# Where the tensors of x, y and h begin in the memory of a decoder-trunk kernel

## What is computed

```python
h = x + 0.5 * swiglu(rms_norm(x, g_ffn1), w_ffn1_gu, w_ffn1_down)      # inner width 2816
u = rms_norm(h, g_mix)
q, k, v, zg, r, us5 = split(u @ w_in)
o    = gated linear attention of q, k, v, zg (chunked recurrence), normed, times silu(r)
o_s5 = diagonal state-space model of us5, gelu, gated
h = h + concat(o, o_s5) @ w_out
h = h + cross_attend(rms_norm(h, g_cross), mem_k, mem_v, w_cq, w_co)
h = h + 0.5 * swiglu(rms_norm(h, g_ffn2), w_ffn2_gu, w_ffn2_down)
y = rms_norm(h, g_final)
```

## The kernel before

| tensor | begins at byte | past a multiple of 128 | past a multiple of 64 |
|---|---|---|---|
| mean_d | 6048 | 32 | 32 |
| gains | 6560 | 32 | 32 |
| eps, one | 6752, 6784 | 96, 0 | 32, 0 |
| h | 6816 | 32 | 32 |
| xh, xl | 25248, 43680 | 32 | 32 |
| yh, yl | 62112, 80544 | 32 | 32 |
| raw | 98976 | 32 | 32 |
| wh, wl | 115360, 123552 | 32 | 32 |
| acc, sq, R, gua, mst | 131744 and on | 32 | 32 |
| AR | 148224 | 0 | 0 |

## Time and profile before

### The profile page before, as it was taken

How to read it: one execution, slowest core, us unless ns; L and a number is a source line. 1 busy time by engine, 2 the same in 40 slices (tenths; PEclk the granted TensorE clock), 3 DMA queues, 4 the chain that set the end, 5 groups by cost and what they waited for, 6 DMA issues and landing times.

```text
span 1282.0 us, 24086 instructions
## 1 busy us (share of the span) xinstructions
PE 1261.7 (98%) x10151; PEld 1218.5 (95%) x10151; DVE 857.1 (67%) x1061; ACT 531.3 (41%) x803; POOL 353.9 (28%) x411
## 2 busy tenths in 40 slices
PE   7999999999999999999999999999999999999997
PEld 6999999999999999999899997599999999999997
DVE  4986479847885636558565437479995589637953
ACT  6644145511224422574443324246553255414543
POOL 0026723288893201000002100032330133102321
PEclk9999999999999999999999999999999999999999
DMA  6233323263223442125333756322332323323322
GB/s 182 81 96 90 91 85 99 83 137 91 74 65 94 91 81 65 51 69 154 119 89 93 232 197 223 122 83 66 100 99 83 99 83 99 91 83 91 87 63 74
DMA packets 221084, 129.94 MB, mean 101 GB/s; under 512 B 22256, under 2 KB 213280, under 8 KB 220960
## 3 DMA queue, kind: packets, MB, share of 16 engines
q1 hardware_dynamic: 217024, 123.83, 33.8%
q10 hardware_dynamic: 3952, 4.58, 1.1%
HBM read 121.42 MB, written 5.78 MB: 99 GB/s over the span
## 4 chain that ended last, share of the span: by engine, by line
PE 92%; DVE 4%; ACT 2%; issue 1%; DMA 1%; SPq 0%; ACTq 0%; DVEq 0%
PE PS L736 89%; PE PS L1361 1%; DMA AR<-in_x_prompt 1%; PE PS L806 0%; ACT wh L1500 0%; ACT gua L1649 0%; DVE Hs L2452 0%; DVE xl L2139 0%; PE PS L1338 0%; DVE AR L2780 0%; PE PS L953 0%; PE PS L1447 0%; DVE ARr L2134 0%; DVE yl L2233 0%; DVE wl L2027 0%
## 5 line engine op out<-in xcount | busy, mean ns | idle before, releaser
L1500 ACT ACTIVATE wh<-raw 128x1024 fp32r<-128x1024 f32 (+1 forms) x126 | 130.1, 1032 | 373.7 <-PE PS L736 373.1
L736 PE MATMUL PS<-yh,wh 128*128 128x288 f32 x960 | 205.6, 296 | 0.0
L736 PE MATMUL PS<-yl,wh 128*128 128x288 f32 x960 | 204.7, 295 | 0.0
L736 PE MATMUL PS<-yh,wl 128*128 128x288 f32 x960 | 204.6, 295 | 0.0
L2027 DVE TENSOR_TENSOR wl<-raw,wh 128x1024 fp32r<-128x1024 f32 (+1 forms) x126 | 154.9, 1229 | 63.7 <-ACT wh L1500 62.3
L736 PE MATMUL PS<-xh,ARr 128*128 128x288 f32 x792 | 174.1, 297 | 0.4 <-ACT sq L1583 0.2
L736 PE MATMUL PS<-xh,wh 128*128 128x288 f32 x736 | 164.4, 305 | 0.1
L736 PE MATMUL PS<-xh,wl 128*128 128x288 f32 x736 | 158.1, 297 | 0.0
L736 PE MATMUL PS<-xl,wh 128*128 128x288 f32 x736 | 157.9, 296 | 0.0
L736 PEld LDWEIGHTS PS<-yh,wh 128*128 128x128 f32 x960 | 154.1, 189 | 1.5 <-DVE yl L2705 0.8
L736 PEld LDWEIGHTS PS<-yh,wl 128*128 128x128 f32 x960 | 154.3, 189 | 0.0
(11 more groups left out here) (378 smaller groups left out, 2183.5 us busy)
## 6 DMA issues: line engine op xcount, KB each, us to landing
raw<-in_w_ffn_gu SPq DMA_DIRECT2D x88, 512.0 KB, 3.9
raw<-in_w_ffn_down SPq DMA_DIRECT2D x32, 512.0 KB, 3.9
raw<-in_w_in SPq DMA_DIRECT2D x16, 512.0 KB, 4.0
raw<-in_w_ckv SPq DMA_DIRECT2D x16, 512.0 KB, 3.8
raw<-in_w_ffn_down SPq DMA_DIRECT2D x16, 384.0 KB, 3.4
Hs<-in_cache_mem_k SPq DMA_DIRECT2D x6, 1024.0 KB, 6.5
raw<-in_w_out SPq DMA_DIRECT2D x8, 512.0 KB, 4.0
raw<-in_w_cq SPq DMA_DIRECT2D x8, 512.0 KB, 4.3
```

Source lines behind the costliest of these rows:

```text
L736: return e.matmul(out, lhsT, rhs, start=start, stop=stop, **kw)
L1500: e.activation(wh[:, n % 2, 0:K * P], raw[:, n % 4, 0:K * P], ACT.Copy).then_inc(w_hi, 1)
```

## The change

The two small constants change their places in the list of tensors. `eps` (32 bytes with rounding) goes ahead of `mean_d`, and `one` (32 bytes) goes from ahead of `h` to behind `raw`. No instruction is added, removed or moved, and no operand changes its size or pattern.

```diff
+        eps = sb("eps", [P, 1])
         mean_d = sb("mean_d", [P, P])
         gains = sb("gains", [P, 6, KD])
-        eps = sb("eps", [P, 1])
-        one = sb("one", [P, 1])
         h = sb("h", [P, KD, T])
         Xs = alias("Xs", 2 * KD * T)
         xh = sb("xh", [P, KD, T], F32R)
...
         yh = sb("yh", [P, KD, T], F32R)
         yl = sb("yl", [P, KD, T], F32R)
         raw = sb("raw", [P, 4, KD * P])
+        one = sb("one", [P, 1])
         wh = sb("wh", [P, 2, KD * P], F32R)
         wl = sb("wl", [P, 2, KD * P], F32R)
```

## The result

| | before | after |
|---|---|---|
| median, 17 runs each | 1284.57 us (1282.56 to 1286.4) | 1286.92 us (1285.42 to 1287.68) |
| ratio | | 1.0016, 95% interval 1.0010 to 1.0022 |
| span of the profiled execution | 1282.0 us | 1285.2 us |

The account below looks back on a forecast made before the run. TensorE's distances between matmul starts were taken as the bound. 2.0 (units) + 5.8 + 0.7 - 1.3 (dense) = 7.2 us off the 1282.0 us span gave 1274.8, with 2.8 for the median 1277.6 us; range 1267 to 1287.5.

Parts of the forecast that it names:

- The bound: Whole kernel: TensorE busy 98% of the span, so the distances between matmul starts make up nearly all the time.
- The third part: All other work on shifted tensors, on ScalarE, VectorE and the loads: counted at nothing.
- What the rows say of starts: Products of a unit: the moving operand's 32 bytes cost 1.6 ns or more a matmul, the stationary operand's nothing.
- The first part: Units: 1188 matmuls go from 133.3 to 131.7 ns, 2.0 us less; 792 streaming from AR unchanged.
- The second part: dense: most matmuls go to 131.7 ns, 5.8 and 0.7 us less; 768 at 130.0 ns lose 1.3 us.
- (c): Rival: dense at 0/32 settles in the slow state, 133.3 ns, throughout; 1285.3 us, chance 0.11.
- (a): Rival: dense falls into the lower rhythm, 130.0 ns, everywhere; 1269.9 us, chance 0.17.
- (d): Rival: operands starting differently within 64 bytes cost time, so dense goes to 134.2 ns; 1289.9 us, chance 0.13.
- (b): Rival: the start doesn't matter and dense keeps its rhythms; 1284.8 us, chance 0.11.
- The rule cited against the change: SBUF reads in 16-byte lines; starts of 32 and 0 both give 72 lines a row, so nothing changes: 1284.8 us.

Follow-up runs that it names:

- maps: Test streams appended behind the last matmul of the kernel before, over pairs of starts of streamed tensor and weights; 131.7 to 133.5 ns a matmul.
- e8: Kernel before with AR alone 128 bytes further on; 1286.71 us, ratio 1.0017.
- e9: Kernel before with eps and one both behind raw, so x, y, h and raw begin 64 bytes earlier; 1281.62 us, ratio 0.9976.
- e2: Kernel before with only yh, yl, raw (and Hs) on a multiple of 128, AR 128 bytes further on; 1286.16 us, ratio 1.0008.
- e5: Kernel before with wh and wl 64 bytes further on, and AR therefore 128; 1282.73 us, ratio 0.9986.
- e3: Kernel before with only h, xh, xl (and Xs) moved to a multiple of 128; 1286.34 us, ratio 1.0012.
- e4: Changed kernel with wh and wl also on a multiple of 128; 1286.29 us, ratio 1.0010 against the kernel before.

## Why the prediction was wrong, point by point

**The bound** was read rightly: TensorE's distances between starts set the time, its two longest waits are 5.2 and 2.5 us, against 5.5 and 2.5 in the earlier trace rows, and nothing on the other engines moved. ScalarE's row and the loads of `raw` of the earlier trace rows read as before (1062 ns against 1059, 3.8 us against 3.9), and VectorE's rows are at 757 and 756 ns again:

```profile
L1500 ACT ACTIVATE wh<-raw 128x1024 fp32r<-128x1024 f32 x110 | 116.8, 1062 | 337.8 <-PE PS L736 337.7
```

```profile
raw<-in_w_ffn_gu SPq DMA_DIRECT2D x88, 512.0 KB, 3.8
```

The third part, counted at nothing, was right.

**The step that failed is the one under "What the rows say of starts"**: that the moving operand's 32 bytes cost 1.6 ns and the stationary one's nothing, read from the products of one unit, and carried over to `dense` ("the pairing of those last two products"). The maps show `dense` at 0/32 and at 32/32 at one pace (133.3 and 133.1 ns), and the kernel does too. In the units the reading fails as well: after the change, products with every operand on a multiple of 128 run at 131.8 and at 133.4 ns side by side, and in e8, where every start within 128 bytes stayed as it was, the last two products went from 132.0 to 133.2 ns. So the 1.6 ns between the products of one unit were not the price of a start within 128 bytes.

What the traces fit instead, in the units, is the distance of the two operands within 256 bytes; no run tests it by itself. The two halves of the tokens begin 1152 bytes (4.5 x 256) apart; `dense` streams both in turn, a product of a unit only one. After the change, the four products whose weights begin 128 bytes away from the streamed tensor within 256 (A11, A12, A22, S3) run at 133.3 to 133.6 ns, the three with no distance (S1, S2, S4) at 131.8 to 132.2. Before, A11 and A12 with 96 bytes ran at 132.9 and 133.4, the last two products with 160 bytes at 132.0 to 132.1; in e9 it is A11 and A12 that have 160, at 132.5 to 132.7, and the last two that have 96, at 132.9 and 133.3. It is not the whole of it: S4 has 96 bytes in e2, e5 and e8 and runs at 132.1 to 132.2, and in 6 of the 33 units of before the last two products ran at 133.2 ns from the same places.

**The first part** (units, 2.0 us less) came out as 0.3 us more. The streams of `xh` gained 0.5 ns instead of 1.65, the 792 "131.7 ns either way: nothing" lost 1.4 ns each, 1.1 us, and the shorter steps between products, which the prediction left out, gave some of it back.

**The second part** (`dense`, 6.5 less 1.3 us) came out as the loss alone, and larger: the groups at 130.0 ns fell to 133.3, not to 131.7, and the rest stayed. In six profiles of before there were 8 such groups, 1.3 an execution or 1.3 x 1.28 = 1.7 us. With the 0.3 us of the units this is 2.0 us, against 2.35 measured between medians (1.3 to 2.8 by the interval). How many fast groups the executions without a profile had, no trace shows.

**The rivals.** (c) had the right paces for `dense`, 133.3 ns throughout and the 130.0 lost, 1285.3 us; it was 1.6 us too low, mainly because it still took the 2.0 us of the units for granted. Its reason, that `dense` is at 0/32, was not the right one: e3 and e8 lose the 130.0 ns with these groups at 32/32. (a) fell: 130.0 ns doesn't become general. (d), unequal starts, fell with the result: `dense` runs at 133.3 ns, not at 134.2, and the same in e4 with equal starts. (b) erred on the two groups. The rule cited against the change, from the Trainium skill's page "SBUF — State Buffer" (16-byte lines, section "Specifications (TRN2)"), gave "no change" and was nearer for `dense` than the forecast. Yet what the prediction drew from it, that starts on multiples of 16 are all alike, doesn't hold: they ran from 131.7 to 133.5 ns in the map, and the measurement decides.

**Open.** Whether the distance within 256 bytes sets the paces inside a unit; what exactly, at the end of a unit, lets a `dense` group fall into 130.0 ns, and what makes a unit slow in one execution and not in the next; and whether a group at 0/32 can take it, since in two profiles with the units kept no slow unit stood ahead of a group. That slow last products go with it is a correlation in the layout of before and with AR 256 bytes on (9 of 9), and it doesn't hold in others (e2, e3, e4, e8, the changed kernel).

## What to carry to other kernels

Where TensorE streams without gaps, read the distance between starts in a stretch before and after, not the listed lengths; and before a stream's pace is put down to one property, such as an operand's start, measure that property alone in that very stream. An effect that a program shows in one profile may be chance: profile the same program two or three times before the difference is built on. For these weight streams it was the distance of the two operands within 128 bytes, and not a round start, that was worth moving (e5 and e9: 64 bytes apart, 132.2 ns, by moving one operand or the other).

## What the hardware showed unexpectedly

At full granted clock, streams of 288 columns in fp32r, each with its own load of weights, kept rhythms that repeat over several matmuls, through whole groups: distances of 132, 128 ns (mean 130.0) in the fast groups of before, of 132, 140, 130, 131 (133.3) in the rest, and after the change of 133, 132, 135, 138, 132, 130, 138, 129 (133.4). The same instructions at the same places could be in the first or in the second over all 384 matmuls of a group. Without other work, the pace of a stream depended on the starts of its two operands: for a streamed tensor at 0 or 32, on the distance of the weights from it, with a period of 128 bytes but for one entry. In the units, AR moved by 128 bytes changed the mean paces and by 256 bytes gave the old ones back.
